# Raw head sums copied out at once, with the division by the denominator moved into the head norm's root

## The chip, the cores and the metric

The kernel runs on one core of a Trainium2 chip, as one program. The metric is the device time of one execution in microseconds, as the median of repeated runs. Several engines of the core work side by side, each through its own queue in order: TensorE (PE in the profile: matrix products, which write the accumulation memory, `ps`, 8 banks of 512 columns), VectorE (DVE), ScalarE (ACT), GpSimd (POOL) and SyncE (SP, which issues DMAs). They wait for each other through semaphores.

## The reference

Three transformer blocks follow each other over 512 tokens of width 1024. The change lies in the third block, in the branch with a matrix memory (four heads of width 256). Cut to what matters, per chunk of the scan:

```python
num = einsum(s, v) + inter * einsum(q, C)
den = sum(s) + inter * einsum(q, n)
h = num / maximum(abs(den), exp(-m_t))
...
mu  = mean(h, axis=-1)
var = mean(square(h - mu), axis=-1)
h   = (h - mu) * rsqrt(var + 1e-6) * hn_g
h   = h * sigmoid(o_pre)
merged = sigmoid(ga) * y_a + sigmoid(gb) * h
```

Because the norm that follows divides by the root of the variance, the division by the denominator d = max(|den|, exp(-m)) can be taken out of h: with raw sums R, h = R/d, and (h - mean h) / sqrt(var h + eps) = (R - mean R) / sqrt(var R + eps d²).

## The kernel before

The kernel keeps everything transposed: a tile is 128 features by 512 tokens. Most of PE's time goes to projections. The class `Line` (matmuls at L574) computes one output tile, a unit, from 8 input chunks with three products each (24 matmuls of 512 columns). Its weights come through a ring of four buffers; ACT copies a unit's weights into the short float form (`hi`, L359), DVE subtracts to get the rest (`lo`, the split, L365), both two units ahead, and PE waits for the split. After each unit ACT takes its result out of the accumulation memory (L3087: gelu or sigmoid, or L951) and DVE multiplies it into place (L3096).

Side work is woven in. Each stage is a generator per engine that yields due times, in units of one projection tile, before each piece of work; `weave` merges all generators of an engine by these times and writes the instructions out in that order. Nothing is reordered at run time. So a due time decides what stands behind what in a queue, and an engine that waits at an instruction holds all behind it.

The third block's side work around the change:
- `ValueTokens`: PE transposes the values (L3316), DVE copies them out (L3324), through bank 2, one group after the other.
- `MemoryGates`: for each head PE spreads a row over the partitions (L3232), DVE subtracts a column (L3264), ACT takes the exponential (L3290), DVE masks (L3270). This gives the decay weights W.
- `Memory`: for head h and key block j (n = 4h + j) PE computes scores (L3354, banks 0 and 1), DVE multiplies them with W into PT (L3418), and PE adds three sums over PT (L3367): the denominator, with a matrix of ones, in bank 3, and the two halves of the head in banks 4 and 5. After j = 3 comes what I call the block: ACT takes |den| into N (L3463), DVE the maximum with EB = exp(-m) (L3425), the reciprocal (L3426) and the two products out of banks 4 and 5 into H (L3427, L3428). PE's next sums wait for this (`head_done`). Then the head's norm: PE sums H over the features (L3390, the mean), DVE centres H (L3437), ACT squares (L3475), PE sums the squares (L3396, the total), ACT takes the root (L3480), DVE the reciprocal of the root (L3442) and scales H with it and the gain (L3444).

ACT holds one table of functions at a time; sigmoid, exponential and root need loads (ACT_TABLE_LOAD) when they alternate. The due times of `Memory`: the block at `when(n) + 0.6`, the norm's mean at `norm_at[h]` = t, centring at t + 0.3, squares at t + 0.5, total at t + 0.7, root at t + 0.95, scaling at t + 1.1.

Of the kernel before, what the change touches and what calls it, by code (L numbers as in the profile page):

```python
# [17 lines left out]
ALU = mybir.AluOpType  # L18
ACT = mybir.ActivationFunctionType
# [14 lines left out]
EPS = 1e-6  # L34
# [189 lines left out]
class Chain:  # L224
# [5 lines left out]
    def do(self, eng, ins):  # L230
        self.value += 1
        ins.then_inc(self.sem, 1)
        eng.wait_ge(self.sem, self.value)
# [3094 lines left out]
class Memory(Stage):  # L3328
# [3 lines left out]
    def __init__(self, core, at, Q, K, VT, EB, H, PT, N, sq, r, conv, gates, tokens, norm_at):  # L3332
        self.core, self.at, self.Q, self.K, self.VT, self.EB, self.H, self.PT, self.N, self.sq, self.r = (
            core, at, Q, K, VT, EB, H, PT, N, sq, r)
        self.conv, self.gates, self.tokens, self.norm_at = conv, gates, tokens, norm_at
        self.scores, self.probs, self.sums = (core.take(n, 16) for n in ("scores", "probs", "out_ready"))
        self.absd, self.done, self.mean, self.centered, self.total, self.root, self.ready = (core.take(n, 4) for n in (
            "norm_abs", "head_done", "head_mean", "head_centered", "head_total", "head_root", "head_ready"))
        self.squared = core.take("head_squared", 8)

    def when(self, n):
# [2 lines left out]
    def tensor(self, pe):  # L3344
        core, T = self.core, SEQ

        def score(n):
            h, j = divmod(n, 4)
            if n == 0:
                pe.wait_ge(self.conv.out.sem, self.conv.out.at(2 * NC))  # L3350
            if n >= 2:
                pe.wait_ge(self.probs.sem, self.probs.at(n - 1))
            for e in range(2):
                last = pe.matmul(core.ps[:, n % 2, 0:T - j * P], self.K[:, 2 * h + e, j * P:(j + 1) * P],  # L3354
                                 self.Q[:, 2 * h + e, j * P:], start=(e == 0), stop=(e == 1))
            last.then_inc(self.scores.sem, 1)

        def add(n):
            h, j = divmod(n, 4)
            pe.wait_ge(self.probs.sem, self.probs.at(n + 1))  # L3360
            if j == 0:
                pe.wait_ge(self.tokens.copied.sem, self.tokens.copied.at(4 * (h // 2) + 4))
                if h:
                    pe.wait_ge(self.done.sem, self.done.at(h))
            p = self.PT[:, n % 2, 0:T - j * P]
            for b, lhs in ((3, core.c("ones")), (4, self.VT[:, j, 2 * h]), (5, self.VT[:, j, 2 * h + 1])):
                last = pe.matmul(core.ps[:, b, j * P:], lhs, p, start=(j == 0), stop=(j == 3))  # L3367
            last.then_inc(self.sums.sem, 1)

        def steps():  # L3370
            yield self.when(0) - 0.35
            score(0)
            for n in range(16):
                if n + 1 < 16:
                    yield self.when(n + 1) - 0.35
                    score(n + 1)
                yield max(self.when(n) + 0.25, self.when(min(n + 1, 15)) - 0.35)
                add(n)

        def norms():  # L3380
            for h in range(4):
                t = self.norm_at[h]
                yield t
                pe.wait_ge(self.done.sem, self.done.at(h + 1))
                if h:
                    pe.wait_ge(self.root.sem, self.root.at(h))
                else:
                    pe.wait_ge(self.gates.arg.sem, self.gates.arg.at(16))
                for e in range(2):
                    last = pe.matmul(core.ps[:, 2, :], core.c("ones"), self.H[:, 2 * h + e], start=(e == 0), stop=(e == 1))  # L3390
                last.then_inc(self.mean.sem, 1)
                yield t + 0.7
                pe.wait_ge(self.centered.sem, self.centered.at(h + 1))
                for e in range(2):
                    pe.wait_ge(self.squared.sem, self.squared.at(2 * h + e + 1))
                    last = pe.matmul(core.ps[:, 2, :], core.c("ones"), self.sq[:, e], start=(e == 0), stop=(e == 1))  # L3396
                last.then_inc(self.total.sem, 1)
        both = [steps(), norms()]
        ahead = [next(p, None) for p in both]
        while any(t is not None for t in ahead):  # L3400
            i = min((t, i) for i, t in enumerate(ahead) if t is not None)[1]
            yield ahead[i]
            ahead[i] = next(both[i], None)

    def vector(self, dve):
        core, T = self.core, SEQ
        do = lambda ins: core.vec.do(dve, ins)

        def steps():
            for n in range(16):  # L3410
                h, j = divmod(n, 4)
                w = T - j * P
                yield self.when(n)
                dve.wait_ge(self.scores.sem, self.scores.at(n + 1))
                dve.wait_ge(self.gates.ready.sem, self.gates.ready.at(n + 1))
                if n >= 2:
                    dve.wait_ge(self.sums.sem, self.sums.at(n - 1))
                dve.scalar_tensor_tensor(out=self.PT[:, n % 2, 0:w], in0=core.ps[:, n % 2, 0:w], scalar=1.0 / 16,  # L3418
                                         in1=self.gates.W(h, j), op0=ALU.mult, op1=ALU.mult).then_inc(self.probs.sem, 1)
                if j < 3:  # L3420
                    continue
                yield self.when(n) + 0.6
                nh = self.N[:, h % 2]
                dve.wait_ge(self.absd.sem, self.absd.at(h + 1))
                do(dve.tensor_tensor(nh, nh, self.EB[:, h], ALU.max))  # L3425
                do(dve.reciprocal(nh, nh))  # L3426
                do(dve.tensor_tensor(self.H[:, 2 * h], core.ps[:, 4, :], nh, ALU.mult))  # L3427
                dve.tensor_tensor(self.H[:, 2 * h + 1], core.ps[:, 5, :], nh, ALU.mult).then_inc(self.done.sem, 1)  # L3428

        def norms():  # L3430
            for h in range(4):
                t = self.norm_at[h]
                H = [self.H[:, 2 * h + e] for e in range(2)]
                yield t + 0.3
                dve.wait_ge(self.mean.sem, self.mean.at(h + 1))
                for e in range(2):
                    ins = dve.scalar_tensor_tensor(out=H[e], in0=core.ps[:, 2, :], scalar=-1.0 / 256, in1=H[e], op0=ALU.mult,  # L3437
                                                   op1=ALU.add)
                ins.then_inc(self.centered.sem, 1)
                yield t + 1.1  # L3440
                dve.wait_ge(self.root.sem, self.root.at(h + 1))
                do(dve.reciprocal(self.r, self.r))  # L3442
                for e in range(2):
                    ins = dve.scalar_tensor_tensor(out=H[e], in0=H[e], scalar=core.p("mlstm_hn_g_3", 2 * h + e), in1=self.r,  # L3444
                                                   op0=ALU.mult, op1=ALU.mult)
                ins.then_inc(self.ready.sem, 1)
        both = [steps(), norms()]
        ahead = [next(p, None) for p in both]
        while any(t is not None for t in ahead):
            i = min((t, i) for i, t in enumerate(ahead) if t is not None)[1]  # L3450
            yield ahead[i]
            ahead[i] = next(both[i], None)

    def scalar(self, act):
        core = self.core

        def steps():
            for h in range(4):
                yield self.when(4 * h + 3) + 0.5
                act.wait_ge(self.sums.sem, self.sums.at(4 * h + 4))  # L3460
                if h >= 2:
                    act.wait_ge(self.done.sem, self.done.at(h - 1))
                act.activation(self.N[:, h % 2], core.ps[:, 3, :], ACT.Abs).then_inc(self.absd.sem, 1)  # L3463

        def norms():
            for h in range(4):
# [6 lines left out]
                    act.wait_ge(self.total.sem, self.total.at(h))  # L3473
                for e in range(2):
                    act.activation(self.sq[:, e], self.H[:, 2 * h + e], ACT.Square).then_inc(self.squared.sem, 1)  # L3475
                yield t + 0.95
                act.wait_ge(self.total.sem, self.total.at(h + 1))
                if h:
                    act.wait_ge(self.ready.sem, self.ready.at(h))
                act.activation(self.r, core.ps[:, 2, :], ACT.Sqrt, bias=core.c("eps6"), scale=1.0 / 256).then_inc(self.root.sem, 1)  # L3480
        both = [steps(), norms()]
        ahead = [next(p, None) for p in both]
        while any(t is not None for t in ahead):
# [128 lines left out]
```

## Time and profile before

| | |
|---|---|
| median of 3 runs | 2823.17 us (2822.75 to 2827.2) |
| profiled execution | 2823.4 us, its span 2821.6 us |
| PE busy | 2661.5 us, 94% of the span, 14358 matmuls |
| DVE busy | 1541.9 us, 55% |
| ACT busy | 1035.8 us, 37% |
| mean granted PE clock | 0.966 of full speed |

The span is what the trace covers; the execution's own time is 1.8 us longer. Busy time of PE is an upper view of its work, since matmuls are pipelined. Where PE is this full, idle time of DVE and ACT costs nothing by itself; it matters only where PE waits for them. A timeline shows the idle time before an operation, and who ended it, in square brackets.

### The profile page before, as it was taken

The page shows a single profiled execution, that of the slowest core. Times are in us where ns is not written, and L with a number is a line of the kernel's source. Part 1 is how long each engine was busy: PE and PEld are TensorE (multiplying, and loading weights), DVE is VectorE, ACT ScalarE, POOL GpSimd, SP SyncE. Part 2 cuts the span into 40 slices and gives each one's busy share as a digit, 9 for nine tenths or more (in the row PEclk, how much of TensorE's full clock was granted, in tenths as well). Part 3 has the DMA queues.
Part 4 walks back from the last instruction along what each step waited for, and adds up shares of the span by engine and source line. Part 5 has one row for each costly group of instructions (what it writes and reads, how often), then busy time and mean ns, then how long its engine had stood idle before and what let it go on. Part 6 is the DMA issues. An engine that isn't in the chain of part 4 may idle for free.

```text
span 2821.6 us, 35708 instructions
## 1 busy us (share of the span) xinstructions
PE 2661.5 (94%) x14358; PEld 2142.8 (76%) x14358; DVE 1541.9 (55%) x2537; ACT 1035.8 (37%) x1807; POOL 331.7 (12%) x270
## 2 busy tenths in 40 slices
PE   7999999999999999998889999989998899899998
PEld 6788888899998867866567777856766578688886
DVE  3787654455445446477647886445743554433444
ACT  3365444433223242234443223343232333322322
POOL 0043310012222010010012221020000000100001
PEclk8999999999999999999889999999999999999999
DMA  3211111122232331320025663322221122223322
GB/s 123 68 46 53 53 61 58 64 83 90 91 96 90 97 120 46 122 65 2 1 87 175 201 194 123 96 95 68 68 67 45 38 82 90 81 91 97 96 92 74
DMA packets 70850, 239.01 MB, mean 85 GB/s; under 512 B 12212, under 2 KB 13109, under 8 KB 70430
## 3 DMA queue, kind: packets, MB, share of 16 engines
q1 hardware_dynamic: 63054, 208.88, 23.3%
q10 hardware_dynamic: 7632, 27.86, 2.9%
q8 instruction: 114, 1.87, 0.3%
q14 instruction: 50, 0.41, 0.0%
HBM read 234.06 MB, written 2.64 MB: 84 GB/s over the span
## 4 chain that ended last, share of the span: by engine, by line
PE 61%; DVE 12%; ACT 3%; issue 2%; POOL 1%; ACTq 0%; DVEq 0%; POOLq 0%
PE ps L574 51%; DVE wl L365 2%; PE ps L2704 2%; ACT wh L359 1%; PE ps L3367 1%; DVE xl L655 1%; PE ps L1770 1%; PE ps L1754 1%; PE ps L1781 1%; DVE arena L3060 1%; DVE arena L1033 1%; PE ps L1619 1%; POOL arena L735 0%; DVE arena L3426 0%; DVE xl L653 0%
## 5 line engine op out<-in xcount | busy, mean ns | idle before, releaser
L574 PE MATMUL ps<-xh,wh 128*128 128x512 f32 (+1 forms) x2728 | 1022.3, 389 | 35.4 <-DVE xl L680 14.8
L574 PE MATMUL ps<-xl,wh 128*128 128x512 f32 (+1 forms) x2728 | 995.0, 379 | 0.0
L574 PE MATMUL ps<-xh,wl 128*128 128x512 f32 (+1 forms) x2728 | 991.2, 378 | 0.0
L365 DVE TENSOR_TENSOR wl<-ring,wh 128x1024 fp32r<-128x1024 f32 x374 | 471.1, 1260 | 650.2 <-ACT wh L359 649.5
L359 ACT ACTIVATE wh<-ring 128x1024 fp32r<-128x1024 f32 x374 | 395.3, 1057 | 992.9 <-PE ps L574 885.3
L574 PEld LDWEIGHTS ps<-xh,wh 128*128 128x128 f32 x2728 | 504.2, 190 | 172.9 <-issue 53.4
L574 PEld LDWEIGHTS ps<-xl,wh 128*128 128x128 f32 x2728 | 502.8, 190 | 100.7 <-issue 9.6
L574 PEld LDWEIGHTS ps<-xh,wl 128*128 128x128 f32 x2728 | 503.9, 191 | 98.3
L2000 PE MATMUL ps<-xh,wh 128*128 128x264 f32 (+1 forms) x816 | 260.4, 319 | 9.6 <-DVE xl L424 9.6
L735 POOL TENSOR_TENSOR arena<-arena 128x512 f32<-128x512 f32 (+1 forms) x42 | 71.5, 1707 | 1422.3 <-ACT arena L719 1422.3
L2000 PE MATMUL ps<-xl,wh 128*128 128x264 f32 (+1 forms) x816 | 235.2, 288 | 0.0
L2000 PE MATMUL ps<-xh,wl 128*128 128x264 f32 (+1 forms) x816 | 235.2, 288 | 0.0
L2000 PEld LDWEIGHTS ps<-xh,wh 128*128 128x128 f32 x816 | 157.6, 193 | 38.4 <-issue 20.7
L2000 PEld LDWEIGHTS ps<-xl,wh 128*128 128x128 f32 x816 | 158.5, 194 | 1.0
L2000 PEld LDWEIGHTS ps<-xh,wl 128*128 128x128 f32 x816 | 158.2, 194 | 0.0
L819 DVE TENSOR_TENSOR h<-ps,h 128x512 f32<-128x512 f32 (+1 forms) x64 | 44.2, 691 | 154.7 <-PE ps L574 154.7
L876 POOL TENSOR_TENSOR arena<-arena 128x516 f32<-128x516 f32 (+1 forms) x44 | 81.1, 1843 | 217.9 <-ACT arena L855 217.9
L863 ACT ACTIVATE arena<-arena 128x512 f32<-128x512 f32 x44 | 27.8, 632 | 203.0 <-DVE arena L895 203.0
L821 DVE SCALAR_TENSOR_TENSOR h<-ps,mod,h 128x512 f32<-128x512 f32 x40 | 30.1, 751 | 113.4 <-PE ps L574 113.4
L879 POOL TENSOR_TENSOR arena<-arena 128x512 f32<-128x512 f32 x44 | 58.4, 1327 | 159.3 <-ACT arena L863 159.3
L655 DVE TENSOR_TENSOR xl<-arena,xh 128x512 fp32r<-128x512 f32 (+1 forms) x108 | 72.2, 727 | 7.6 <-ACT xh L645 7.6
L1033 DVE CUSTOM_DVE_ANT_0 arena<-arena 128x1024 f32<-128x1024 f32 x48 | 69.8, 1489 | 0.0
(386 smaller groups left out, 2790.7 us busy)
## 6 DMA issues: line engine op xcount, KB each, us to landing
ring<-in_weights SPq DMA_DIRECT2D x374, 512.0 KB, 3.5
arena<-in_w_ada ACTq DMA_DIRECT2D x48, 512.0 KB, 4.6
arena<-in_cmp_w SPq DMA_DIRECT2D x2, 2048.0 KB
h<-in_x ACTq DMA_DIRECT2D x4, 528.0 KB, 6.3
arena<-strip_scratch SPq DMA_DIRECT2D x8, 264.0 KB, 3.7
out_features<-arena SPq DMA_DIRECT2D x8, 256.0 KB, 2.1
con<-in_consts SPq DMA_DIRECT2D x1, 777.0 KB, 11.1
arena<-in_c ACTq DMA_DIRECT2D x1, 512.0 KB, 3.6
```

The lines of the kernel that those rows point to most:

```text
L359: act.activation(flat(self.wh[:, s % 2]), flat(self.ring[:, s % RING]), ACT.Copy).then_inc(self.hi_ready, 1)
L365: dve.tensor_tensor(flat(self.wl[:, s % 2]), flat(self.ring[:, s % RING]), flat(self.wh[:, s % 2]).bitcast(F32), ALU.subtract).then_inc(se ...
L574: last = pe.matmul(self.place(u, e), w[:, k, :], x[:, k, o:o + m], start=(k == 0 and i == 0), stop=(k == self.chunks - 1 and i == 2))
L655: ins = dve.tensor_tensor(xl, a, xh, ALU.subtract)
L735: pool.tensor_tensor(self.acc, self.sq[:, 0] if k == 1 else self.acc, self.sq[:, k % 2], ALU.add).then_inc(self.added.sem, 1)
L819: ins = dve.tensor_tensor(out, self.got(u), out, ALU.add)
L821: ins = dve.scalar_tensor_tensor(out=out, in0=self.got(u), scalar=self.scale[u], in1=out, op0=ALU.mult, op1=ALU.add)
L876: pool.tensor_tensor(g, g, self.r_gate, ALU.mult).then_inc(self.gate_scaled.sem, 1)
L879: pool.tensor_tensor(self.mid[:, j, 2], self.mid[:, j, 2], self.r, ALU.mult).then_inc(self.scaled.sem, 1)
L1033: dve.tensor_tensor_reduce(out=w, in0=w, in1=self.spread, scale=1.0, scalar=0.0, op0=ALU.mult, op1=ALU.add, accum_out=self.parts[:, (n + e ...
L2000: last = pe.matmul(self.place(e), w[:, k, :], x[:, k, o:o + m], start=(k == 0 and n == 0), stop=(k == NC - 1 and n == 2))
L2704: last = pe.matmul(core.ps[:, self.place(n) + e, 0:c], w[:, k, :], x[:, k, o:o + c], start=(k == lo and i == 0), stop=(k == hi - 1 and i = ...
```

## The change

After the last sums of a head, DVE waits for the sums themselves and copies banks 4 and 5 raw into H. Later (a due time 0.4 on) it takes the maximum d into N and turns it into d² x 1e-6. The mean, centring and squares work on raw sums. DVE then adds total/256 to N, and bounds the result by 1e-36 from below (`head_varied`); ACT takes the root of N, without the bias. PE's next sums wait for the copies and for the Abs, since bank 3 is now read apart from them. The root on ACT is due at t + 1.2, the two new DVE operations at t + 1, the scaling at t + 1.4. The Abs of head h waits for the root of head h - 2, because N holds its data until then. Names in the diff: `absd` is the semaphore norm_abs, `done` head_done, `floor` and `varied` are new.

```diff
@@ -3336,6 +3336,7 @@
         self.scores, self.probs, self.sums = (core.take(n, 16) for n in ("scores", "probs", "out_ready"))
         self.absd, self.done, self.mean, self.centered, self.total, self.root, self.ready = (core.take(n, 4) for n in (
             "norm_abs", "head_done", "head_mean", "head_centered", "head_total", "head_root", "head_ready"))
+        self.floor, self.varied = core.take("head_floor", 4), core.take("head_varied", 4)
         self.squared = core.take("head_squared", 8)
 
     def when(self, n):
@@ -3362,6 +3363,7 @@
                 pe.wait_ge(self.tokens.copied.sem, self.tokens.copied.at(4 * (h // 2) + 4))
                 if h:
                     pe.wait_ge(self.done.sem, self.done.at(h))
+                    pe.wait_ge(self.absd.sem, self.absd.at(h))
             p = self.PT[:, n % 2, 0:T - j * P]
             for b, lhs in ((3, core.c("ones")), (4, self.VT[:, j, 2 * h]), (5, self.VT[:, j, 2 * h + 1])):
                 last = pe.matmul(core.ps[:, b, j * P:], lhs, p, start=(j == 0), stop=(j == 3))
@@ -3383,7 +3385,7 @@
                 yield t
                 pe.wait_ge(self.done.sem, self.done.at(h + 1))
                 if h:
-                    pe.wait_ge(self.root.sem, self.root.at(h))
+                    pe.wait_ge(self.varied.sem, self.varied.at(h))
                 else:
                     pe.wait_ge(self.gates.arg.sem, self.gates.arg.at(16))
                 for e in range(2):
@@ -3420,12 +3422,15 @@
                 if j < 3:
                     continue
                 yield self.when(n) + 0.6
+                dve.wait_ge(self.sums.sem, self.sums.at(4 * h + 4))
+                for e in range(2):
+                    ins = dve.tensor_copy(self.H[:, 2 * h + e], core.ps[:, 4 + e, :])
+                ins.then_inc(self.done.sem, 1)
                 nh = self.N[:, h % 2]
+                yield self.when(n) + 1
                 dve.wait_ge(self.absd.sem, self.absd.at(h + 1))
                 do(dve.tensor_tensor(nh, nh, self.EB[:, h], ALU.max))
-                do(dve.reciprocal(nh, nh))
-                do(dve.tensor_tensor(self.H[:, 2 * h], core.ps[:, 4, :], nh, ALU.mult))
-                dve.tensor_tensor(self.H[:, 2 * h + 1], core.ps[:, 5, :], nh, ALU.mult).then_inc(self.done.sem, 1)
+                dve.scalar_tensor_tensor(out=nh, in0=nh, scalar=EPS, in1=nh, op0=ALU.mult, op1=ALU.mult).then_inc(self.floor.sem, 1)
 
         def norms():
             for h in range(4):
@@ -3437,7 +3442,13 @@
                     ins = dve.scalar_tensor_tensor(out=H[e], in0=core.ps[:, 2, :], scalar=-1.0 / 256, in1=H[e], op0=ALU.mult,
                                                    op1=ALU.add)
                 ins.then_inc(self.centered.sem, 1)
-                yield t + 1.1
+                yield t + 1
+                dve.wait_ge(self.total.sem, self.total.at(h + 1))
+                dve.wait_ge(self.floor.sem, self.floor.at(h + 1))
+                nh = self.N[:, h % 2]
+                do(dve.scalar_tensor_tensor(out=nh, in0=core.ps[:, 2, :], scalar=1.0 / 256, in1=nh, op0=ALU.mult, op1=ALU.add))
+                dve.tensor_scalar(nh, nh, 1e-36, None, ALU.max).then_inc(self.varied.sem, 1)
+                yield t + 1.4
                 dve.wait_ge(self.root.sem, self.root.at(h + 1))
                 do(dve.reciprocal(self.r, self.r))
                 for e in range(2):
@@ -3459,7 +3470,7 @@
                 yield self.when(4 * h + 3) + 0.5
                 act.wait_ge(self.sums.sem, self.sums.at(4 * h + 4))
                 if h >= 2:
-                    act.wait_ge(self.done.sem, self.done.at(h - 1))
+                    act.wait_ge(self.root.sem, self.root.at(h - 1))
                 act.activation(self.N[:, h % 2], core.ps[:, 3, :], ACT.Abs).then_inc(self.absd.sem, 1)
 
         def norms():
@@ -3473,11 +3484,11 @@
                     act.wait_ge(self.total.sem, self.total.at(h))
                 for e in range(2):
                     act.activation(self.sq[:, e], self.H[:, 2 * h + e], ACT.Square).then_inc(self.squared.sem, 1)
-                yield t + 0.95
-                act.wait_ge(self.total.sem, self.total.at(h + 1))
+                yield t + 1.2
+                act.wait_ge(self.varied.sem, self.varied.at(h + 1))
                 if h:
                     act.wait_ge(self.ready.sem, self.ready.at(h))
-                act.activation(self.r, core.ps[:, 2, :], ACT.Sqrt, bias=core.c("eps6"), scale=1.0 / 256).then_inc(self.root.sem, 1)
+                act.activation(self.r, self.N[:, h % 2], ACT.Sqrt).then_inc(self.root.sem, 1)
         both = [steps(), norms()]
         ahead = [next(p, None) for p in both]
         while any(t is not None for t in ahead):
```

In the changed kernel the copies are L3427, the maximum L3432, the square L3433, the addition L3449, the bound from below L3450, the root L3491, its reciprocal L3453 and the scalings L3455.

How the written order moves is shown at three places. First DVE, at the end of head 0's sums (L3324 is the copy of turned values for which PE waits; L3418, in the change L3420, the probability product; the names in brackets are semaphores). Before:

```order
L3324 COPY arena<-ps 128x512 [waits probs_turned]
L3425 TENSOR_TENSOR arena<-arena 128x512 [waits norm_abs]
L3426 RECIPROCAL arena<-arena 128x512 [waits vector_step]
L3427 TENSOR_TENSOR arena<-ps,arena 128x512 [waits vector_step]
L3428 TENSOR_TENSOR arena<-ps,arena 128x512 [waits vector_step]
L3324 COPY arena<-ps 128x512 [waits probs_turned]
L365 TENSOR_TENSOR wl<-ring,wh 128x1024 [waits weights_hi_ready]
```

And in the change:

```order
L3324 COPY arena<-ps 128x512 [waits probs_turned]
L3427 COPY arena<-ps 128x512 [waits out_ready]
L3427 COPY arena<-ps 128x512
L3324 COPY arena<-ps 128x512 [waits probs_turned]
L3432 TENSOR_TENSOR arena<-arena 128x512 [waits norm_abs]
L3433 SCALAR_TENSOR_TENSOR arena<-arena 128x512 [waits vector_step]
L365 TENSOR_TENSOR wl<-ring,wh 128x1024 [waits weights_hi_ready]
```

Two copies that wait for the sums alone stand where four operations stood; the maximum and the square have moved behind L3324.

Second, DVE at the end of head 1's sums, among the gate weights of head 3 (L3264). Before:

```order
L3264 TENSOR_SCALAR arena<-ps,arena 128x512 [waits m_rows]
L3425 TENSOR_TENSOR arena<-arena 128x512 [waits norm_abs]
L3426 RECIPROCAL arena<-arena 128x512 [waits vector_step]
L3427 TENSOR_TENSOR arena<-ps,arena 128x512 [waits vector_step]
L3428 TENSOR_TENSOR arena<-ps,arena 128x512 [waits vector_step]
L3264 TENSOR_SCALAR arena<-ps,arena 128x384
L3264 TENSOR_SCALAR arena<-ps,arena 128x256
L365 TENSOR_TENSOR wl<-ring,wh 128x1024 [waits weights_hi_ready]
```

And in the change:

```order
L3264 TENSOR_SCALAR arena<-ps,arena 128x512 [waits m_rows]
L3427 COPY arena<-ps 128x512 [waits out_ready]
L3427 COPY arena<-ps 128x512
L3264 TENSOR_SCALAR arena<-ps,arena 128x384
L3264 TENSOR_SCALAR arena<-ps,arena 128x256
L3432 TENSOR_TENSOR arena<-arena 128x512 [waits norm_abs]
L3433 SCALAR_TENSOR_TENSOR arena<-arena 128x512 [waits vector_step]
L365 TENSOR_TENSOR wl<-ring,wh 128x1024 [waits weights_hi_ready]
```

The two subtractions for the gate weights come ahead of the maximum and the square.

Third, ACT in head 0's norm (L3475 and L3486 are the squares, L3480 and L3491 the root, L3463 and L3474 the Abs of head 2). Before:

```order
L3475 ACTIVATE arena<-arena 128x512
L3480 ACT_TABLE_LOAD
L3480 ACTIVATE arena<-ps,con 128x512 [waits head_total]
L359 ACTIVATE wh<-ring 128x1024 [waits weights_used,weights_arrived1]
L3087 ACT_TABLE_LOAD
L3087 ACTIVATE arena<-ps 128x512 [waits multiplied]
L3463 ACTIVATE arena<-ps 128x512 [waits head_done,out_ready]
```

And in the change:

```order
L3486 ACTIVATE arena<-arena 128x512
L359 ACTIVATE wh<-ring 128x1024 [waits weights_used,weights_arrived1]
L3087 ACTIVATE arena<-ps 128x512 [waits multiplied]
L3491 ACT_TABLE_LOAD
L3491 ACTIVATE arena<-arena 128x512 [waits head_varied]
L3474 ACTIVATE arena<-ps 128x512 [waits head_root,out_ready]
```

The root now stands behind the next weight copy and its sigmoid, and waits for DVE. PE's order is the same in both; only its waits differ.

## Rows read from the trace of the kernel before

**Rows 1.** The page: the chain that ended last, share of the span by engine

```profile
PE 61%; DVE 12%; ACT 3%; issue 2%; POOL 1%; ACTq 0%; DVEq 0%; POOLq 0%
```

**Rows 2.** Busy time by stretch: us, each engine's busy us (instructions), granted clock, DMA share, GB/s

```profile
2110.00:2310.00 200.00, 178.51 (x685) 127.45 (x684) 94.15 (x108) 63.73 (x78) 0.00 (x0) 0.95 0.17 53
```

**Rows 3.** Timeline of PE, start us, duration: each operation before which PE stood idle

```profile
2149.53 1.11 PE L3316 MATMUL ps<-con,arena 128*128 128x128 f32 x4 [5.45 <-DVE arena L3324]
...
2176.80 1.25 PE L3232 MATMUL ps<-arena,con 4*128 4x512 f32 x2 [2.73 <-DVE arena L3264]
...
2197.72 2.08 PE L3367 MATMUL ps<-arena,con 128*128 128x512 f32 x2 [7.39 <-DVE arena L3418]
...
2235.17 1.59 PE L3367 MATMUL ps<-arena,con 128*128 128x512 f32 x2 [2.59 <-DVE arena L3418]
...
2253.11 0.70 PE L3367 MATMUL ps<-arena,con 128*128 128x256 f32 x2 [1.46 <-DVE arena L3418]
...
2267.31 1.96 PE L3396 MATMUL ps<-arena,con 128*128 128x512 f32 x4 [1.88 <-ACT arena L3475]
```

**Rows 4.** Busy time by stretch, columns as in rows 2: behind stalls 1 to 5

```profile
2149.50:2154.20 4.70, 4.67 (x14) 3.89 (x15) 2.91 (x4) 0.00 (x0) 0.00 (x0) 0.54 0.35 112
...
2176.80:2183.20 6.40, 6.40 (x18) 4.48 (x19) 1.59 (x5) 0.88 (x3) 0.00 (x0) 0.73 0.16 65
...
2197.70:2202.50 4.80, 4.78 (x7) 2.22 (x8) 0.83 (x3) 0.00 (x0) 0.00 (x0) 0.60 0.06 26
...
2235.20:2239.70 4.50, 4.50 (x7) 1.96 (x8) 1.57 (x3) 2.43 (x3) 0.00 (x0) 0.62 0.31 109
...
2253.10:2257.00 3.90, 3.89 (x17) 3.29 (x18) 0.15 (x1) 0.82 (x1) 0.00 (x0) 1.00 0.00 0
```

**Rows 5.** Chain of waits, 2110 to 2310 us: start us, length us, what

```profile
2119.08 2.58 PE ps L3367 x6
...
2235.17 4.54 PE ps L3367 x6
```

**Rows 6.** Timeline of ACT and DVE, start us, duration: head 0's block and behind it

```profile
2142.72 0.60 ACT L3463 ACTIVATE arena<-ps 128x512 f32<-128x512 f32 x1 [6.51 <-PE ps L3367]
...
2148.79 0.68 DVE L3324 COPY arena<-ps 128x512 f32<-128x512 f32 x1
```

**Rows 7.** Timeline of ACT and DVE: head 1's block and behind it

```profile
2185.58 0.60 ACT L3463 ACTIVATE arena<-ps 128x512 f32<-128x512 f32 x1 [7.89 <-PE ps L3367]
...
2191.66 1.00 DVE L3264 TENSOR_SCALAR arena<-ps,arena 128x384 f32<-128x384 f32 x2
...
2192.73 1.04 ACT L359 ACTIVATE wh<-ring 128x1024 fp32r<-128x1024 f32 x1
```

**Rows 8.** Timeline of DVE: root of head 0, then head 2's block to the split

```profile
2222.54 3.35 DVE L3442 RECIPROCAL arena<-arena 128x512 f32<-128x512 f32 x1
...
2227.25 0.68 DVE L3425 TENSOR_TENSOR arena<-arena 128x512 f32<-128x512 f32 x1
...
2232.69 1.22 DVE L365 TENSOR_TENSOR wl<-ring,wh 128x1024 fp32r<-128x1024 f32 x1
```

**Rows 9.** Timeline of ACT and DVE: in front of the squares at head 3

```profile
2265.14 0.58 ACT L3087 ACTIVATE arena<-ps 128x512 f32<-128x512 f32 x1
...
2265.23 1.28 DVE L3437 SCALAR_TENSOR_TENSOR arena<-ps,arena 128x512 f32<-128x512 f32 x2
```

**Rows 10.** Timeline of ACT and DVE: behind head 0's total; last, the next weight copy

```profile
2217.45 0.69 ACT L3480 ACTIVATE arena<-ps,con 128x512 f32<-128x512 f32 x1 [4.71 <-PE ps L3396]
...
2218.93 1.06 ACT L359 ACTIVATE wh<-ring 128x1024 fp32r<-128x1024 f32 x1 [0.80 <-PE ps L574]
...
2220.01 1.28 ACT L3087 ACT_TABLE_LOAD   x1
...
2220.02 1.23 DVE L365 TENSOR_TENSOR wl<-ring,wh 128x1024 fp32r<-128x1024 f32 x1 [5.30 <-ACT wh L359]
...
2226.91 1.06 ACT L359 ACTIVATE wh<-ring 128x1024 fp32r<-128x1024 f32 x1 [0.19 <-PE ps L574]
```

## The prediction

> **What bounds the kernel now.** I went from the whole to the place. First the page: TensorE (PE) holds 61% of the chain that ended last, VectorE (DVE) 12% [rows 1], so a change pays only where PE stands still or runs at its lower clock. Then the table by stretches: the memory attention of the third block lies between about 2110 and 2310 us, and PE is busy 178.51 of those 200 us, so 21.5 us are idle [rows 2]. The timeline of PE shows all of this in six places, each with its length and the engine that ended it: 5.45 us at L3316, 2.73 at L3232, 7.39, 2.59 and 1.46 at L3367, and 1.88 at L3396 [rows 3]. I call them stalls 1 to 6. Their sum is 21.50 us.
>
> The stalls cost more than their length. The stretches behind stalls 1 to 4 have a mean granted clock of 0.54, 0.73, 0.60 and 0.62, that behind stall 5 has 1.00 [rows 4]. A clock of 0.54 as a mean is a mixture of the two levels 1.2 and 2.4 GHz. Length times missing clock gives the price: 4.70 x 0.46 = 2.16 us behind stall 1, 6.40 x 0.27 = 1.73 behind 2, 4.80 x 0.40 = 1.92 behind 3, 4.50 x 0.38 = 1.71 behind 4. The chain of waits checks the last one: the same six passes of L3367 take 2.58 us at full clock and 4.54 behind stall 4, so 1.96 us [rows 5]. I use 1.96 there. At full recovery the stage could give 21.5 + 7.8 = 29.3 us; nothing outside the stage is touched.
>
> **The change part by part.** Before, when a head's sums are complete, DVE waits for |den| from ScalarE (ACT), takes the maximum, a reciprocal of 3.35 us (that of the root is of the same form [rows 8]), and two products out of PSUM. After, it copies the two banks at once, and makes max and square later. The order shows what stands behind this block in DVE's queue in each head; that decides which stall shortens.
>
> *Head 0, stall 1.* PE waits for the copy L3324, which stands right behind the block. The sums were ready when the Abs on ACT started, at 2142.72; L3324 started at 2148.79 [rows 6]. The two new copies are ops of L3324's own kind, PSUM to SBUF, 0.68 us each; two such DVE ops in a row start 0.60 apart (1.28 us for two at L3437 [rows 9]). So L3324 can start at 2142.72 + 1.20 = 2143.92, 4.87 us earlier. Stall 1 falls from 5.45 to 0.58. The price of 2.16 us of low clock goes with it, because even a stall of 1.46 us left the clock at 1.00 [rows 3, 4].
>
> *Gate weights, stall 2.* PE waits for the last piece of L3264, which waits behind a weight split and a product whose times come from ACT's chain. No op of the change stands between. It stays: 0.
>
> *Head 1, stall 3.* Behind the block stand two L3264, then split, products and the probability product L3418 that PE waits for. The sums were ready at 2185.58, the first L3264 started at 2191.66 [rows 7]. Now it starts after two copies, at 2186.78: 4.88 us earlier. ACT's exponential and its L359 at 2192.73 follow it without idle time, and everything to L3418 hangs on those; the chain moves as a whole. Max and square (about 1.3 us) now stand behind the two L3264, where DVE would wait for ACT anyway: the split waits for L359 (1.04 us from 2192.73), so before it came 2.1 us after the first L3264. Stall 3 falls from 7.39 to 2.51. As stall 4 with 2.59 us was followed by low clock, I leave its price in the sum: 0 from the clock.
>
> *Head 2, stall 4.* Heads are counted from 0. The block runs from 2227.25 to the split at 2232.69, 5.44 us [rows 8], and PE's product stands behind it. Now: two copies 1.20, then max and square, ops between SBUF tiles like L3425, which takes 0.68 [rows 8]; each waits for the one before, which adds 0.03 or so: 0.72 each. That is 2.64 us, 2.80 saved. Stall 4 was 2.59: gone, with only 0.2 us to spare. Low clock behind it, 1.96 us, goes too.
>
> *Head 1's norm, stall 5.* This stall comes from the root's reciprocal and two scalings in front of a probability product. They stay, but the change makes the chain from total to root longer: L3449 and L3450 (0.69 us each at most; L3450 has one source and may cost anything from nothing to that) between total and root. Bounds: DVE stands idle 5.30 us before the split at 2220.02 [rows 10], from 2214.72, and the total is there when the old root starts, 2217.45. Both ops end by 2218.87, before the split's source is ready. That is root 0; root 1 has the same neighbours. ACT now does hi, sigmoid (0.58), table load (1.28) and root (0.69 at most): with hi (1.06) from 2218.93 that is 2222.54 at the latest [rows 9, 10]. The reciprocal started at 2222.54 [rows 8]. So the root comes no later: 0, and stall 5 stays.
>
> *Head 3, stall 6.* PE waits for the squares of head 2's norm, which came after head 3's block and the centring (2265.23 [rows 9]). Copies first and max and square behind the centring bring that forward by more than 3 us, but the squares also stand behind ACT's sigmoid, which ended at 2265.14 + 0.58 = 2265.72 [rows 9]. The first square may overlap its end a little and takes about 0.6 us, so PE can go at 2266.35, not 2267.31. Saved 0.96, of 1.88.
>
> *New waits.* PE's first sum matmul of a head now waits for the Abs of the head before as well. ACT has it 0.6 us after the sums, PE comes a head later. ACT's Abs of head 2 stands behind the root of head 0: it needs 0.6 us more, and PE comes for it after the whole of head 2. Cost 0, hidden by the projection matmuls. DMAs and SP's queue do not change, nor does POOL's.
>
> **Sum.** Stalls: 4.87 + 4.88 + 2.59 + 0.96 = 13.3 us. Clock: 2.16 + 1.96 = 4.1. Together 17.4 us less in the profiled execution's own time of 2823.4: **2806.0 us**. The median of the runs, 2823.17, is 0.2 us from it, and I make no correction.
>
> **The clock behind stall 3.** The rows show low clock behind 2.59, 2.73, 5.45 and 7.39 us of idle PE and full clock behind 1.46 [rows 3, 4]; 2.51 is a little shorter than the shortest that cost something. The Trainium skill, page "TensorE: Matmul & The Clock Gate", section "The HAM clock gate (the "warmup" mystery)", says the monitor runs free of the program, so the same idle stretch may or may not be punished. By that rule stall 3 could come through at full clock, and the sum would be 19.3, not 17.4; the trace, with four stalls that paid and one that didn't, can't refute it.
>
> **The rivals.** Within 0.2% (5.6 us) is about what a measurement of this kernel can't tell from no change.
> - *Full clock behind the shortened stall 3.* Mechanism: 2.51 us of idle is below every stall that paid. For: 2.59 is close. Against: 2.59 and 2.73 both paid. Another 1.92 us go: 2804.1. Chance 0.12.
> - *Head 1's chain doesn't move.* If ACT's L359 has to wait for its unit of matmuls, the exponentials come no earlier and stall 3 stays at up to 7.39. For: ACT takes three other jobs there (two table loads, a sigmoid). Against: in the row L359 follows without idle time. The sum loses 4.88: 2810.9. Chance 0.06.
> - *The waits move.* ACT's root waits for DVE now, and the Abs of heads 2 and 3 stand behind it; if a root is late, PE stands at the first sums of head 3 and at the projection behind it. It takes 17.4 / 2 = 8.7 us in each of two heads to give all back: about 2823. Against: root 0 is on time above. Chance 0.05.
> - *Slower.* In DVE's queue L3449 waits for the total and holds the weight split behind it, which PE needs for its next projection unit. The point from which it decides: the split at 2220.02 is needed only when the unit before it ends; ACT's next hi, which starts at such an end, ran at 2226.91 in the trace [rows 10], so L3449 would have to be some 5 us late. If that were so in every head, PE would wait for the serial chain of total, L3449, L3450, table load, root, reciprocal and scalings: 0.72 + 0.69 + 1.28 + 0.69 + 3.35 + 1.28 (two DVE ops in a row) = 8.01 us, 32.0 in four heads, less the 17.4: 2838.0. The idle 5.30 us speaks against it. Chance 0.03.
> That the change doesn't do what it says is excluded: the four reciprocals of the division are gone from the order.
>
> **How the numbers follow.** The forecast has 0.74, the rivals 0.12, 0.06, 0.05 and 0.03. The likeliest case alone reaches from 2804.5 (L3450 cheap, stall 3's clock partly back) to 2808.5 (stall 4 comes back with 0.5 us and some low clock). The range 2803.0 to 2811.5 takes in the first two rivals; it leaves out 0.08 and some misses of size. Faster by over 0.2%: 0.74 + 0.12 + 0.06 = 0.92; within 0.2%: 0.05; slower: 0.03.
>
> **What would show it.** In the profile after: no L3426-like reciprocal in steps, PE's idle before L3316 about 0.6 us, before the first L3367 of head 2 (L3369 after) about 2.5, none or under 0.5 in head 3, 1.5 at head 3's third sum, 0.9 before the squares' sum, L3232 unchanged at 2.7. Low clock behind two stalls, not four. The prediction is wrong if the sum of idle PE in this stage is above 12 us, if a stall ended by the norm_abs or by a split appears, or if low clock shows behind stalls under 1 us.

## The result and the profile after

The changed kernel takes 2802.57 us as a median of 11 executions (2793.84 to 2815.41), the kernel before 2822.75 us over as many (2813.45 to 2844.3). The ratio is 0.992, with a 95% interval of 0.9899 to 0.9942. Timed once more over 6 executions (run rep_after_timed) it was 0.9936 (0.992 to 0.9951). So it is faster, by 0.8% in the first comparison and 0.6% in the second, the way that was forecast. The median lies 3.4 us under the forecast of 2806.0 and 0.4 us under the lower end of the range, 2803.0: the range didn't hold it. The forecast was worked out from the profiled execution of the kernel before; that of the changed kernel took 2803.22 us, just inside the range.

Its span is 2801.4 us. PE is busy 171.85 of the 180 us in which the stage now lies, so 8.15 us are idle, where [rows 2] had 21.5. By stretches (columns as in [rows 2]):

```profile
2110.00:2290.00 180.00, 171.85 (x680) 123.85 (x679) 86.91 (x116) 62.03 (x77) 0.00 (x0) 0.99 0.19 58
```

The timeline of PE in the kernel after, each operation before which it stood idle (answers to [rows 3]; L3369 is the old L3367, L3398 the old L3396):

```profile
2143.64 0.66 PE L3316 MATMUL ps<-con,arena 128*128 128x128 f32 x4 [0.58 <-DVE arena L3324]
...
2168.97 1.12 PE L3232 MATMUL ps<-arena,con 4*128 4x512 f32 x2 [2.73 <-DVE arena L3264]
...
2184.99 1.13 PE L3369 MATMUL ps<-arena,con 128*128 128x512 f32 x2 [2.52 <-DVE arena L3420]
...
2233.87 0.70 PE L3369 MATMUL ps<-arena,con 128*128 128x256 f32 x2 [1.37 <-DVE arena L3420]
...
2247.11 1.96 PE L3398 MATMUL ps<-arena,con 128*128 128x512 f32 x4 [0.94 <-ACT arena L3486]
```

Stall by stall, before, forecast and after: stall 1 5.45, 0.58, 0.58 us; stall 2 2.73, 2.73, 2.73; stall 3 7.39, 2.51, 2.52; stall 4 2.59, 0, 0; stall 5 1.46, 1.46, 1.37; stall 6 1.88, 0.92, 0.94. Every length came out within 0.1 us of the forecast.

Granted clock behind stalls 1, 2 and 3, kernel after (answers to [rows 4]):

```profile
2143.60:2148.40 4.80, 4.76 (x20) 3.36 (x21) 4.21 (x6) 1.83 (x2) 0.00 (x0) 1.00 0.27 62
...
2168.90:2175.30 6.40, 6.33 (x18) 4.56 (x19) 1.61 (x6) 0.94 (x3) 0.00 (x0) 0.73 0.18 69
...
2185.00:2189.80 4.80, 4.80 (x16) 2.96 (x17) 0.80 (x3) 0.00 (x0) 0.00 (x0) 1.00 0.06 23
```

Here is the difference. Behind stall 3 I had left the low clock in the sum; PE runs at 1.00 there, so low clock stands behind one stall, not two. Five pieces of the chain of waits, kernel after, show the stage's length, this price and what stands in place of stall 4 (start us, length us):

```profile
2118.07 2.58 PE ps L3369 x6
...
2144.30 2.09 PE ps L574 x9
...
2184.99 2.84 PE ps L3369 x6
...
2217.97 2.58 PE ps L3369 x6
...
2266.80 1.72 PE ps L3398 x4
```

In the kernel before, the first sums are those at 2119.08 [rows 5]; the last total and the pieces behind stalls 1 and 3 are:

```profile
2150.64 3.58 PE ps L574 x9
...
2197.72 4.74 PE ps L3367 x6
...
2286.98 1.72 PE ps L3396 x4
```

I call the time from the start of the first sums to the start of the last total the stage: 2286.98 - 2119.08 = 167.90 us before, 2266.80 - 2118.07 = 148.73 after, 19.2 less. Idle time is 13.4 of it (4.87 + 4.87 + 2.59 + 0.09 + 0.94). The rest is clock, with a little restart: behind stall 1 4.69 became 2.75 us (L3316 with nine L574; L3316's lengths, 1.11 and 0.66, are in the timelines), behind stall 3 4.74 became 2.84, behind stall 4 4.54 became 2.58. Together 5.8 us. Of this about 0.26 us behind stall 4 isn't clock but the restart that any stall brings (2.84 us for these six sums behind a stall at full clock, 2.58 without one). The two profiled executions differ by 20.2 us; the last 1.0 us lies in front of the stage, which began 1.0 us earlier.

### The profile page after: what moved, and what is told of

Its sections match the earlier page's. It is cut to its first block, busy times and chain, and to the rows that moved or that the text cites. A ratio compares the mean times of both kernels' runs of the same rounds, so it can differ in the third digit from the quotient of the medians.

```text
span 2801.4 us, 35722 instructions
## 1 busy us (share of the span) xinstructions
PE 2656.1 (95%) x14358; PEld 2138.5 (76%) x14358; DVE 1534.5 (55%) x2545; ACT 1034.4 (37%) x1806; POOL 332.6 (12%) x270
## 4 chain that ended last, share of the span: by engine, by line
PE 63%; DVE 11%; ACT 3%; issue 2%; POOL 1%; ACTq 0%; DVEq 0%; POOLq 0%
PE ps L574 52%; DVE wl L365 2%; PE ps L2704 2%; ACT wh L359 1%; PE ps L3369 1%; DVE xl L655 1%; PE ps L1770 1%; PE ps L1754 1%; PE ps L1781 1%; DVE arena L3060 1%; DVE arena L1033 1%; PE ps L3355 1%; PE ps L1619 1%; POOL arena L735 0%; DVE xl L653 0%
## 5 line engine op out<-in xcount | busy, mean ns | idle before, releaser
L574 PE MATMUL ps<-xh,wh 128*128 128x512 f32 (+1 forms) x2728 | 1021.2, 389 | 34.5 <-DVE xl L680 13.9
L574 PE MATMUL ps<-xl,wh 128*128 128x512 f32 (+1 forms) x2728 | 993.9, 379 | 0.0
L574 PE MATMUL ps<-xh,wl 128*128 128x512 f32 (+1 forms) x2728 | 989.9, 377 | 0.0
L574 PEld LDWEIGHTS ps<-xh,wh 128*128 128x128 f32 x2728 | 503.2, 190 | 172.3 <-issue 53.1
L574 PEld LDWEIGHTS ps<-xl,wh 128*128 128x128 f32 x2728 | 502.3, 190 | 100.8 <-issue 9.7
L574 PEld LDWEIGHTS ps<-xh,wl 128*128 128x128 f32 x2728 | 503.3, 191 | 99.0
```

The source lines that it names most:

```text
L574: last = pe.matmul(self.place(u, e), w[:, k, :], x[:, k, o:o + m], start=(k == 0 and i == 0), stop=(k == self.chunks - 1 and i == 2))
```

## The experiments

In all of them "stage" is meant as above; the kernel before has 167.90 and 168.03 us in two traces, the changed one 148.73, 148.80 and 148.75 in three. Behind the last total the length is the same: in all 13 traces, 534.6 to 534.7 us are left to the end of the span. So what two traces differ by outside the stage lies in front of it. The runs other than `best` and the retimed change are single executions, and they are compared by the stage.

### Both kernels once more

> The kernel before once more, for the spread of the granted clock between executions. Idle times of PE in the memory stage should come out as in the first trace to 0.1 us (5.45, 2.73, 7.39, 2.59, 1.46, 1.88). Theory A, the length of a stall decides: low clock behind the four stalls of 2.59 us and more, at prices as before (2.0, 1.8, 2.2, 2.0 us by the chain). Theory B, the chip's watch runs free of the program: the two stalls of 2.6 to 2.7 us pay in one execution and not in another, the ones of 5.45 and 7.39 pay always; the time differs from the first by several us with the same idle times.

> The changed kernel once more. Idle times as in its first trace to 0.1 us (0.58, 2.73, 2.52, 0, 1.37, 0.94). Theory A: low clock behind the stall of 2.73 and none behind 2.52, as in the first trace. Theory B: either may pay about 1.9 us, and the span outside the stage differs from the first trace by a few us as well.

The kernel before took 2828.12 us this time, the changed one 2803.08. Two pieces of the chain of waits, kernel before, second trace, behind stall 4 and the last total:

```profile
2239.90 4.54 PE ps L3367 x6
...
2291.73 1.72 PE ps L3396 x4
```

And the changed kernel's second trace, behind stall 3:

```profile
2184.80 2.84 PE ps L3369 x6
```

The idle times are those of the first traces to 0.04 us, and every price of low clock to 0.1 us: low clock behind four stalls before, behind stall 2 alone after. What stands in one trace of this stage stood in the next, for both kernels; theory B in its plain form falls inside the stage. The times differ elsewhere. The second trace of before entered the stage at 2123.70, 4.6 us later than the first. Its clock between 1200 and 1500 us (columns as in [rows 2]):

```profile
1200.00:1300.00 100.00, 89.82 (x593) 64.64 (x592) 68.92 (x181) 38.50 (x107) 12.34 (x29) 0.88 0.14 43
1300.00:1400.00 100.00, 90.50 (x788) 62.38 (x787) 70.87 (x257) 45.19 (x133) 5.15 (x16) 0.82 0.01 1
1400.00:1500.00 100.00, 87.01 (x397) 61.51 (x398) 47.68 (x89) 49.81 (x93) 12.71 (x8) 0.89 0.22 69
```

In the first trace these three were 0.91, 0.85 and 0.91. This stretch lies ahead of the stage, and the change doesn't touch it. Of the 13 traces, ten have 0.90 or 0.91 between 1200 and 1300 us and enter the stage between 2116.80 and 2119.72; three have 0.88 and enter between 2123.48 and 2126.05. So most of the scatter between the profiled executions goes with this stretch. The executions without a profile can't be looked into.

### One head at a time

The edit keeps the old block for the heads that aren't in `new`, with its waits and due times:

```diff
+        self.new = (0,)
...
                 yield self.when(n) + 0.6
+                if h not in self.new:
+                    nh = self.N[:, h % 2]
+                    dve.wait_ge(self.absd.sem, self.absd.at(h + 1))
+                    do(dve.tensor_tensor(nh, nh, self.EB[:, h], ALU.max))
+                    do(dve.reciprocal(nh, nh))
...
```

> The new scheme for head 0 alone, the old division for heads 1 to 3. My sum: stall 1 from 5.45 to 0.6, the other five unchanged to 0.2 us; 4.9 us of idle time less, and 2.0 of low clock behind it, 7 us in all against the kernel before. Rival, the gain hangs together over the heads (a head that comes early only waits longer at the next): stalls 2 or 3 grow by what stall 1 loses.

> The new scheme for head 1 alone. My sum: stall 3 from 7.39 to 2.5, the others unchanged to 0.2 us. The low clock behind stall 3 costs 2 us more or not: Theory A (length, with the threshold between 2.52 and 2.59) says not; Theory B says it may. Rival: the exponentials wait for the unit of matmuls behind ACT's weight copy, stall 3 stays above 5.

> The new scheme for head 2 alone. My sum: stall 4 gone (2.59 to 0), the others unchanged to 0.2 us, and the 1.96 us of low clock behind it gone: the stage, from the first sums to the last total, 4.5 us shorter than the 168.0 us of the two traces of before. Rival: stall 4 is only passed on to stall 5 or 6, and these grow by as much; the stage is less than 2.5 us shorter.

*Head 0* took 2816.08 us, the stage 2279.70 - 2118.62 = 161.08, so 6.9 less; forecast 7. Stall 1 is 0.58. *Head 1* took 2823.69 us, but this execution entered the stage late, at 2126.05; the stage is 2287.27 - 2126.05 = 161.22, 6.7 less: 4.87 of idle time and 1.9 of clock (stall 3 is 2.52 us, and the six sums behind it take 2.84, first line below). The single time would have said "no gain". *Head 2* took 2819.33 us, the stage 2282.90 - 2117.63 = 165.27, only 2.7 less where I expected 4.5. Stall 4 is gone and stalls 5 and 6 have their lengths, so it isn't passed on as idle time. The chain of waits, first head 1 alone, one piece:

```profile
2199.95 2.84 PE ps L3374 x6
```

Head 2 alone, and last the kernel before, behind its stall 6:

```profile
2117.63 2.57 PE ps L3374 x6
...
2261.52 3.44 PE ps L3406 x4
2264.96 12.04 PE ps L574 x51
...
2282.90 1.72 PE ps L3406 x4
```

```profile
2269.27 11.82 PE ps L574 x51
```

The piece at 2261.52 stands behind stall 6 (1.91 us, as before the change). It takes 3.44 us, where it took 1.96 in [rows 3], and the 51 passes behind it take 12.04 us for 11.82: the low clock has moved from stall 4 to stall 6, and costs 1.7 us there. This is one trace. The three heads add up to 16.3 us; the whole change gives 19.2, as it shortens stall 6 too (head 3's block, 0.94 us) and this price falls due nowhere.

The run with head 0 alone holds the other half of the question. Its stall 4, in front of head 3's sums, was 2.51 us long. The timeline of PE and the clock behind it:

```profile
2227.84 1.44 PE L3374 MATMUL ps<-arena,con 128*128 128x512 f32 x2 [2.51 <-DVE arena L3428]
```

```profile
2227.80:2232.30 4.50, 4.46 (x7) 1.93 (x8) 1.64 (x3) 2.43 (x3) 0.00 (x0) 0.62 0.29 113
```

The same length as stall 3 of the changed kernel to 0.01 us, and here it pays: 4.54 us for six sums that take 2.84 there. Length alone doesn't decide (theory A falls).

### Maximum and square not set apart

```diff
                 nh = self.N[:, h % 2]
-                yield self.when(n) + 1
                 dve.wait_ge(self.absd.sem, self.absd.at(h + 1))
```

> The change, but maximum and square stand directly behind the two copies, in front of the copy L3324 and of the gate subtractions. My sum: each costs 1.3 us there; stall 1 from 0.58 to 1.9, stall 3 from 2.52 to 3.8, and low clock behind stall 3 (1.9 us): 4.5 us longer than the stage of the change, 153.2 against 148.8. Rival (the split of the block into two pieces is worth nothing, since DVE waits afterwards anyway): stalls as in the change.

It took 2810.83 us, the stage 2274.41 - 2119.72 = 154.69. The stage is 5.9 us longer than the change's 148.76, where I expected 4.5. Stall 1 is 1.91 us, stall 3 3.84, both as expected, so the later due time is worth 2.6 us of idle time (the rival falls). The chain of waits behind both:

```profile
2147.28 3.18 PE ps L574 x9
2150.46 1.80 PE ps L3355 x4
...
2190.93 4.14 PE ps L3369 x6
2195.08 3.85 PE ps L574 x15
```

At full clock these take 2.09, 1.29, 2.84 and 3.50. So stall 1 with 1.91 us paid 1.6 us of clock, which I hadn't expected, and stall 3 1.65. Idle time and clock make the whole 5.9.

### The gate weights earlier

```diff
             for j in range(4):
-                yield self.when(h, j)
+                yield self.when(h, j) - (0.1 * j if h >= 2 else 0)
                 if j == 0:
                     dve.wait_ge(self.m_spread.sem, self.m_spread.at(h + 1))
```

> The change, and the gate subtractions of heads 2 and 3 are due 0.1 apart, not 0.2, so that they stand ahead of the next weight split. My sum: stall 2 gone (2.73) with its 1.8 us of low clock, stall 3 from 2.52 to 1.4, as the exponentials start before the block: 5.6 us off the stage, 143.2. Rival: the exponentials wait for ACT, which has the weight copy and table loads in the same order as before; stall 2 goes, stall 3 grows by as much.

The stage is 2266.69 - 2123.48 = 143.21 us, the forecast to 0.01. Stall 2 is gone, stall 3 1.31, so the rival falls: stall 3 didn't grow. The execution took 2803.11 us, since it entered the stage 5.4 us later than the changed kernel's first trace, with the low clock of 0.88, 0.82 and 0.89 between 1200 and 1500 us.

### A stall with nothing in front of it

The gates kernel with two more copies in head 1 (`gates_pad`), and with one (`gates_pad1`):

```diff
+                if h == 1:
+                    for _ in range(2):
+                        do(dve.tensor_copy(self.H[:, 2 * h], core.ps[:, 4, :]))
                 for e in range(2):
                     ins = dve.tensor_copy(self.H[:, 2 * h + e], core.ps[:, 4 + e, :])
```

> As the one before, and in head 1 two more copies of bank 4 into the same place stand in front of the two real ones (0.7 us each), which brings stall 3 to 2.6 to 2.8 us while no stall stands before it. It asks why a stall of 2.52 us behind head 1 ran on at full clock in three traces, while one of 2.51 to 2.59 behind head 2 was followed by low clock in four. Theory C, what PE did before decides: without the low stretch of stall 2 just before, stall 3 is now followed by low clock (1.9 us more). Theory D, the length decides: a stall under 2.59 is not followed by low clock, one of 2.6 or more is; then both this stall and every stall of this length pay.

> As gates_pad, with one extra copy, so that stall 3 is 2.0 us with no stall of more than 0.6 us before it. In the change 2.52 us at this place, behind stall 2 and its low stretch, cost no clock. Theory C, what PE did before decides: 2.0 us here is followed by low clock all the same (1 to 2 us), as 2.76 was. Theory E, it takes more than 2.52 us at this place, whatever went before: full clock, and the stage is 143.2 + 0.7 = 143.9 us.

With two copies stall 3 was 2.76 us and paid 1.4 (the six sums took 4.24 us, the stage 2264.29 - 2118.25 = 146.04); as that length pays elsewhere too, it told C and D not apart. With one copy it was 2.04 us. The timeline and the granted clock, one copy:

```profile
2181.11 2.04 PE L3369 MATMUL ps<-arena,con 128*128 128x512 f32 x2 [2.04 <-DVE arena L3420]
```

```profile
2181.10:2185.60 4.50, 4.49 (x7) 1.97 (x8) 0.83 (x3) 0.00 (x0) 0.00 (x0) 0.62 0.26 100
```

The six sums take 4.54 us, and the stage 2264.65 - 2119.00 = 145.65, where theory E had 143.9. A stall of 2.04 us pays 1.7 us at the very place where 2.52 us paid nothing in four traces (three of the changed kernel, one of head 1 alone). What differs is what PE did before: in those four, stall 2 stood before, and its low stretch had ended some 9 us earlier. Theory E falls, and C is the one that fits. It rests on one trace with each number of copies; that these two paid by chance isn't excluded, though no repeat of a kernel changed the pattern in this stage. Nor is such a low stretch a safeguard: in the run before, a stall 3 of 3.84 us paid 1.65 us behind the same stall 2. Whether the low stretch or the stall in front of it is what protects, and why, isn't shown.

### A version that beats both

Besides the gates' due times, two others move:

```diff
-                yield t + 1.4
+                yield t + (1.45 if h == 1 else 1.4)
                 dve.wait_ge(self.root.sem, self.root.at(h + 1))
...
-                yield t + 0.5
+                yield t + (0.4 if h == 2 else 0.5)
                 act.wait_ge(self.centered.sem, self.centered.at(h + 1))
```

> The change with three due times moved: gate subtractions of heads 2 and 3 closer together (as in the run gates), the scaling of head 1's norm 0.05 later so that it stands behind the probability product, the squares of head 2's norm 0.1 earlier so that they stand ahead of the weight copy. My sum against the change: stall 2 (2.73 and 1.8 of low clock), stall 3 down by 1.2, stall 5 (1.4 and 0.25 of restart) and stall 6 (0.94 and 0.25) gone: the stage falls from 148.8 to 140.4 us, the time by 8 us. Rival: the low clock only moves, as it did to stall 6 in the run only2; the stall of 1.3 us that is left, or one outside the stage, pays 1 to 2 us, and the stage is 142 or more.

> The change itself, timed beside the run best on the same chip. The ratio to the kernel before should be 0.992 to 0.994; the stage in its trace 148.8 us.

The median of 6 executions is 2794.94 us (2785.54 to 2802.66), the ratio to the kernel before 0.9896 (0.9875 to 0.9916); the changed kernel beside it had 2803.33 and 0.9936. So 8.4 us less than the change, forecast 8. In its trace PE stands idle at two places in the stage. The timeline of PE:

```profile
2144.61 0.66 PE L3316 MATMUL ps<-con,arena 128*128 128x128 f32 x4 [0.58 <-DVE arena L3324]
...
2180.43 1.12 PE L3369 MATMUL ps<-arena,con 128*128 128x512 f32 x2 [1.31 <-DVE arena L3420]
```

The chain of waits at both ends of the stage:

```profile
2119.04 2.58 PE ps L3369 x6
...
2259.41 1.72 PE ps L3398 x4
```

The stage is 140.37 us, forecast 140.4, with no low clock left, so the rival falls: the low clock didn't move to another stall. The three due times moved together; what each gives by itself was measured for the gates alone.

## Why the prediction was right, and where it failed

- *What bounds the stage*: right. All of the gain lies where PE stood idle or slow; the code behind the stage gives nothing (534.6 us in both), and the 1.0 us of 20.2 in front of it lies in code that the change doesn't touch.
- *Head 0, stall 1*: right, 0.58 us; the clock's price of 2.16 us came back as 1.94. The reason given, that even 1.46 us left the clock at 1.00, holds for 0.58 us but has a narrow margin: 1.91 us at this place paid 1.6 in the run with maximum and square in front.
- *Stall 2*: right, unchanged to 0.01 us, and its clock too.
- *Head 1, stall 3*: the length right, 2.52 for 2.51; ACT's chain moved as a whole. **The step that failed** is its clock: "I leave its price in the sum: 0 from the clock." It is the term of the sum that was mis-sized: 1.9 us went (4.74 us became 2.84). I took the price by the length of the stall from its neighbour, stall 4; the runs show that a stall's length alone doesn't set it. The rival "full clock behind the shortened stall 3", at 0.12, is what happened, and its sum was 2804.1. I had also counted the rows wrongly: "four stalls that paid and one that didn't" leaves out stall 6, whose 1.88 us cost no clock either (the sums behind it take 1.96 us, of which 0.24 is restart). The reason that I gave for that rival, a length below every stall that paid, is refuted too: 2.51, 2.04 and 1.91 us paid in other runs. From the Trainium skill, page "TensorE: Matmul & The Clock Gate", section "The HAM clock gate (the "warmup" mystery)", I cited that the monitor runs free of the program. That stalls of like length may or may not be punished was my inference from it, and these rows agree with that. The page also says that the count of slow matmuls varies from run to run; this stage doesn't show that (the same prices in every repeat).
- *Head 2, stall 4*: right, gone. The sum had only 0.2 us to spare; in the trace the product ends at 2217.51 and PE starts on it at 2217.97, so it was some 0.4. Alone, this head would have given 2.7 us, not 4.5, as the low clock goes over to stall 6.
- *Stall 5*: right (1.37 for 1.46). L3450 takes 0.43 us, within its bounds, and the root came no later. But what the reciprocal of the root waits for has changed: before, it followed L3096; after, it stands idle 0.60 us for ACT's root. Counted from the start of ACT's weight copy, it comes after 3.52 us where it came after 3.61, so the new chain fits with 0.1 us to spare. The prediction had both at 3.61.
- *Stall 6*: right, 0.94 for 0.92. ACT's sigmoid bounds it: in the chain of waits the squares start as it ends, at 2246.44, and in the last version, with the squares ahead of it, the stall is gone.
- *New waits*: none of them binds; no stall ended by the Abs or a split appears. The two rivals that rest on such waits are refuted by the timeline, and so is the one by which head 1's chain doesn't move (stall 3 would have stayed at up to 7.39 us).
- *The sum* was 17.4 us, the stage shows 19.2. With the right clock it would have been 19.3. The remaining 1.0 us is scatter in front of the stage, and that the median lies 0.65 us under the profiled execution is scatter too.
- *The range* was made from the terms of the change alone. Executions of the changed kernel lie between 2793.84 and 2815.41, and scatter of several us from outside the stage, such as the 4.6 us between two traces of the kernel before, belongs to every time. A lower end of 2803.0 stood only 1.1 us under a rival that I had given a chance, and left no room for this. So the miss of the range is the clock's 1.9 us together with scatter: the clock alone would have left 2804.1, inside it.

## What to carry to other kernels

Read off, for each stall of the engine that bounds, which instruction ends it and what stands in front of that one in its queue; removing work from there gains its own length, and at most the length of the stall. Here six stall lengths came out of such sums to 0.1 us. The clock behind a stall isn't such a term: keep it as a spread of its own (0 to 2 us for each stall of about 2 to 3 us), and remember that a stall removed may put its price on the next one. Where executions scatter by 10 us, compare the stage between two landmarks in the traces, not the times.

## What the runs showed of the hardware beyond that

Behind a stall of PE the granted clock fell to the lower of its two levels for part of the next 4 to 5 us, at a price of 1.4 to 2.1 us, or not at all. It was paid after 1.91 us (twice), 2.04, 2.51, 2.59, 2.73, 2.76, 3.84, 5.45 and 7.39 us of idle time, and not after 0.58 to 1.50, nor after 1.88 to 1.91 (in four traces) or 2.52 to 2.54 (in four). The two kernels that were traced again showed the same pattern in every repeat; what PE did before the stall is what differed where the pattern did. A restart alone costs about 0.25 us: six sums took 2.84 us behind a stall at full clock, and 2.58 without one.
